# Compression contracted over 128 rows and log gates with split terms in one product, with three orders moved

## The reference, cut to what matters

```python
# compression: 31 blocks of 32 positions, 16 apart, for 2 groups of 64 channels
blocks = t[:, :, idx_c] + pe                     # (B, G, 31, 32, 64)
flat = blocks.reshape(B, G, n_cmp, L * DH)       # 32 * 64 = 2048 long
return jax.nn.silu(flat @ w1) @ w2               # w1: 2048 x 64
...
# log gates of the linear attention: rank 16
log_a = jax.nn.log_sigmoid((a_lr @ w_alpha2 + b_alpha).astype(jnp.float32)) / GLA_TAU
b = jnp.cumsum(heads(log_a, GLA_DK), axis=3)
```

## Time and profile before

| | before |
|---|---|
| median of 3 runs | 1480.3 us (1478.27 to 1482.73) |
| profiled execution, its own time | 1477.46 us |
| its span | 1475.7 us |
| PE busy | 1464.4 us (99%), 7260 matmuls |
| PEld busy | 1182.3 us (80%) |
| DVE, ACT, POOL busy | 664.9, 584.3, 653.6 us |
| granted clock | 1.0 over the whole span |

### The profile page before, as it was taken

How to read it: one execution, slowest core, us unless ns; L and a number is a source line. 1 busy time by engine, 2 the same in 40 slices (tenths; PEclk the granted TensorE clock), 3 DMA queues, 4 the chain that set the end, 5 groups by cost and what they waited for, 6 DMA issues and landing times.

```text
span 1475.7 us, 19987 instructions
## 1 busy us (share of the span) xinstructions
PE 1464.4 (99%) x7260; PEld 1182.3 (80%) x7260; DVE 664.9 (45%) x1081; ACT 584.3 (40%) x919; POOL 653.6 (44%) x304
## 2 busy tenths in 40 slices
PE   9999999999999999999999999999999999999999
PEld 7888888888878877888888886777678888888887
DVE  5214655775544276333340107988665333333000
ACT  5133332765563344333232225666654322332221
POOL 4434312772244434444444542666234444444543
PEclk9999999999999999999999999999999999999999
DMA  5522211111123222333323333321123332333333
GB/s 196 160 86 83 75 57 58 43 58 44 58 86 100 87 84 88 98 99 99 93 92 112 102 104 119 120 72 60 41 74 98 100 96 90 98 99 100 100 106 123
DMA packets 38495, 135.07 MB, mean 92 GB/s; under 512 B 4496, under 2 KB 4752, under 8 KB 38176
## 3 DMA queue, kind: packets, MB, share of 16 engines
q1 hardware_dynamic: 37248, 130.70, 27.8%
q10 hardware_dynamic: 1184, 3.51, 0.7%
HBM read 132.09 MB, written 2.10 MB: 91 GB/s over the span
## 4 chain that ended last, share of the span: by engine, by line
PE 78%; issue 13%; DVE 4%; POOL 4%; ACT 0%; DMA 0%; POOLq 0%; SPq 0%; DVEq 0%
PE bank L1149 17%; PE bank L1151 17%; PE bank L1150 17%; POOL wL L479 3%; PE bank L1500 3%; PE bank L1502 3%; PE bank L1501 3%; PE bank L1178 2%; PE bank L1180 2%; PE bank L1179 2%; DVE bank L2229 1%; PE bank L1279 1%; PE bank L1280 1%; PE bank L1281 1%; PE bank L1555 1%
## 5 line engine op out<-in xcount | busy, mean ns | idle before, releaser
L479 POOL TENSOR_TENSOR wL<-raw,wH 128x1024 fp32r<-128x1024 f32 x234 | 573.8, 2452 | 766.7 <-ACT wH L575 628.4
L575 ACT ACTIVATE wH<-raw 128x1024 fp32r<-128x1024 f32 x209 | 221.3, 1059 | 592.0 <-PE bank L1151 526.4
L1149 PE MATMUL bank<-aH,wH 128*128 128x512 f32 x920 | 359.8, 391 | 1.1 <-POOL wL L479 1.1
L1150 PE MATMUL bank<-aL,wH 128*128 128x512 f32 x920 | 358.0, 389 | 0.0
L1151 PE MATMUL bank<-aH,wL 128*128 128x512 f32 x920 | 358.0, 389 | 0.0
L1149 PEld LDWEIGHTS bank<-aH,wH 128*128 128x128 f32 x920 | 172.7, 188 | 40.7 <-POOL wL L479 2.1
L1151 PEld LDWEIGHTS bank<-aH,wL 128*128 128x128 f32 x920 | 172.7, 188 | 36.2
L1150 PEld LDWEIGHTS bank<-aL,wH 128*128 128x128 f32 x920 | 172.7, 188 | 35.9 <-issue 0.5
L1151 PE MATMUL bank<-fH,wL 128*128 128x512 f32 x352 | 137.0, 389 | 0.0
L1150 PE MATMUL bank<-fL,wH 128*128 128x512 f32 x352 | 137.0, 389 | 0.0
L1149 PE MATMUL bank<-fH,wH 128*128 128x512 f32 x352 | 136.9, 389 | 0.0
(11 more groups left out here) (332 smaller groups left out, 2010.0 us busy)
## 6 DMA issues: line engine op xcount, KB each, us to landing
raw<-in_w SPq DMA_DIRECT2D x234, 512.0 KB, 3.3
bmk<-in_bias SPq DMA_DIRECT2D x6, 512.0 KB, 4.6
out_x<-xT SPq DMA_DIRECT2D x8, 256.0 KB, 4.4
xT<-in_x SPq DMA_DIRECT2D x3, 512.0 KB, 7.3
ct<-in_ct ACTq DMA_DIRECT2D x3, 384.0 KB, 4.2
w1k<-in_w1k ACTq DMA_DIRECT2D x1, 1024.0 KB, 6.0
w1v<-in_w1v ACTq DMA_DIRECT2D x1, 1024.0 KB, 5.0
xT<-in_x SPq DMA_DIRECT2D x2, 256.0 KB, 3.5
```

The lines of the kernel that those rows point to most:

```text
L479: pool.tensor_tensor(wL[:, c_slot, :], raw[:, c_slot, :], wH[:, c_slot, :].bitcast(F32), ALU.subtract).then_inc(sem("w_lo"), 1)
L575: act.activation(wH[:, s, :], raw[:, s, :], ACT.Copy).then_inc(sem("w_hi"), 1)
L1149: pe.matmul(bank[:], hi, H[:, ka, :], start=(k == 0), stop=False)
L1150: pe.matmul(bank[:], hi, L[:, ka, :], start=False, stop=False)
```

## The change

The compression contracts two positions at once: the first 16 positions of a block lie in rows 0 to 63 and the last 16 in rows 64 to 127, so that 16 products over 128 rows replace 32 over 64 rows for each tensor and group. Both groups now use all rows and differ only in the partitions (columns of the array) that they write. `kin` is filled in eight DVE operations of 64 partitions. PE's values of group 4 are interleaved with the compression: keys, one chunk, values, one chunk, two log gates, two chunks.

The log gates become one product each in the rounded type: rows 0 to 15 hold the high parts of weight and input, rows 32 to 47 the low part of the weight by the high part of the input, rows 64 to 79 the weight rounded again by the low part of the input, the other rows zeros. ACT makes the high parts (three copies) and DVE the low parts (two subtractions) ahead of time.

In three places an order moves: on ACT in `swiglu`, `ahead(p, 1, 1)` goes ahead of `silu(0, 1)`; on DVE in the grid loop, `normed(2, 1)` goes ahead of three taps; behind the loop, `low_of_conv(3)` goes ahead of `masked_max(13)`.

```diff
@@ act, in1
+            act.wait_ge(sem("small_landed"), 16 * 5)
+            act.activation(alpha_w[0:ALPHA_ROWS], wa2, ACT.Copy).then_inc(sem("alpha_split"), 1)
+            for row in ALPHA_AT[0:2]:
+                act.activation(alpha_x[row:row + 32], pj[0:32, MISC, :], ACT.Copy).then_inc(sem("alpha_split"), 1)
             group(p, 12)
+            group(p, 16, 1)
             act.wait_ge(sem("cmp_hid"), 1)
...
+            group(p, 17, 1)
             log_gate(0)
             log_gate(1)
-            group(p, 16, 2)
-            act.wait_ge(sem("kin_ready"), 4)
+            group(p, 18, 1)
+            act.wait_ge(sem("kin_ready"), 8)
             act.wait_ge(sem("v_S"), 2)
             high_of_keys(0)
+            group(p, 19, 1)
             high_of_keys(1)
-            group(p, 18, 2)
             group(p, 20)
@@ act, swiglu
                     high_f(0, 0)
+                    ahead(p, 1, 1)
                     silu(0, 1)
-                    ahead(p, 1, 1)
                     high_f(0, 1)
@@ pe, in1
-            for i, w1 in enumerate((w1k, w1v)):
-                for l in range(CL):
-                    for g in range(NG):
-                        r = slice(g * DH, (g + 1) * DH)
-                        mm = pe.matmul(B[7][r, i * 64:i * 64 + NCMP], w1[r, l, :], kin[i][r, l, :],
-                                       start=(l == 0), stop=(l == CL - 1))
-            mm.then_inc(sem("cmp_hid"), 1)
+            def hidden_of_blocks(i, w1):
+                for b in range(CST):
+                    for g, rows in enumerate(group_rows):
+                        mm = pe.matmul(B[7][rows, i * 64:i * 64 + NCMP], w1[:, b, :], kin[:, i, b, g, :],
+                                       start=(b == 0), stop=(b == CST - 1))
+                return mm
             def log_gate(h):
-                pe.matmul(B[ALPHA_BANK[h]][:], wa2[:, h * DK:(h + 1) * DK], pj[0:RANK, MISC, :], start=True, stop=True)\
-                    .then_inc(sem("alpha_z"), 1)
+                pe.matmul(B[ALPHA_BANK[h]][:], alpha_w[0:ALPHA_ROWS, h * DK:(h + 1) * DK], alpha_x[0:ALPHA_ROWS, :],
+                          start=True, stop=True).then_inc(sem("alpha_z"), 1)
+            hidden_of_blocks(0, w1k)
+            values_by_token(4, range(0, 2))
+            hidden_of_blocks(1, w1v).then_inc(sem("cmp_hid"), 1)
+            values_by_token(4, range(2, 4))
             pe.wait_ge(sem("v_S"), 2)
+            pe.wait_ge(sem("alpha_split"), 5)
             log_gate(0)
             log_gate(1)
-            values_by_token(4)
+            values_by_token(4, range(4, KD))
@@ dve, in1
-                    dve.tensor_tensor(kin[i][:, a * CST:(a + 1) * CST, :], src, pos, ALU.add).then_inc(sem("kin_ready"), 1)
+                    for g, rows in enumerate(group_rows):
...
+                        dve.tensor_tensor(kin[group_rows[a], i, :, g, :], src, pos, ALU.add).then_inc(sem("kin_ready"), 1)
...
+            dve.wait_ge(sem("alpha_split"), 3)
+            row = ALPHA_AT[1]
+            dve.tensor_tensor(alpha_w[row:row + 32], wa2[row:row + 32], alpha_w[row:row + 32].bitcast(F32), ALU.subtract)\
+                .then_inc(sem("alpha_split"), 1)
+            dve.tensor_tensor(alpha_x[ALPHA_AT[2]:ALPHA_ROWS], pj[0:32, MISC, :], alpha_x[0:32].bitcast(F32), ALU.subtract)\
+                .then_inc(sem("alpha_split"), 1)
...
+            values_by_token(4)
             dve.memset(attnT[:], 0.0).then_inc(sem("attn_zero"), 1)
-            values_by_token(4)
@@ dve, in2
+                if SPREAD_AT.get(t) == 2:
+                    normed(2, 1)
                 taps(left)
-                if t in SPREAD_AT:
+                if SPREAD_AT.get(t, 2) < 2:
                     normed(SPREAD_AT[t], 1)
...
             silu_of_conv(3)
+            low_of_conv(3)
             masked_max(13)
-            low_of_conv(3)
```

More of the change, by code:

```diff
@@ L34 @@
 GH, DK, DV, RANK, TAU, CH = 4, 128, 256, 16, 16.0, 64
+ALPHA_AT, ALPHA_ROWS = (0, 32, 64), 96
 NCH = S // CH
@@ L239, in two_blocks_kernel @@
         spare = sb("spare", [P, S], F32, sc1)
-        wa2 = spare[0:RANK, :]
+        wa2 = spare[0:ALPHA_ROWS, :]
         kcx = sb("kcx", [P, NG, 2 * NCP], F32R, sc1)
         with ExitStack() as early:
[L243 to L246, removed]
+            sb("under_kin", [P, 2, S], F32, early)
+            kin = sb("kin", [P, 2, CST, NG, NCMP], F32, early)
+            w1k = sb("w1k", [P, CST, DH], F32, early)
+            w1v = sb("w1v", [P, CST, DH], F32, early)
+            sb("under_alpha", [P, 576], F32, early)
+            alpha_w = sb("alpha_w", [P, S], F32R, early)
+            alpha_x = sb("alpha_x", [P, S], F32R, early)
         with ExitStack() as gla:
@@ L1266, in _, with values_by_token @@
             mm.then_inc(sem("nr_T"), 1)
-            def values_by_token(g):
-                for k in range(KD):
+            def values_by_token(g, ks=range(KD)):
+                for k in ks:
                     q = p.c0 + 4 * g + k // 2
@@ L1286, in _ @@
             pe.wait_ge(sem("small_landed"), 16 * 5)
-            pe.wait_ge(sem("kin_ready"), 4)
+            pe.wait_ge(sem("kin_ready"), 8)
             pe.wait_ge(sem("v_root"), 1)
-            for i, w1 in enumerate((w1k, w1v)):
-                for l in range(CL):
-                    for g in range(NG):
-                        r = slice(g * DH, (g + 1) * DH)
-                        mm = pe.matmul(B[7][r, i * 64:i * 64 + NCMP], w1[r, l, :], kin[i][r, l, :],
-                                       start=(l == 0), stop=(l == CL - 1))
-            mm.then_inc(sem("cmp_hid"), 1)
-            def log_gate(h):
-                pe.matmul(B[ALPHA_BANK[h]][:], wa2[:, h * DK:(h + 1) * DK], pj[0:RANK, MISC, :], start=True, stop=True)\
-                    .then_inc(sem("alpha_z"), 1)
+            def hidden_of_blocks(i, w1):
[4 more added lines that the diff above has]
+                return mm
+            def log_gate(h):
+                pe.matmul(B[ALPHA_BANK[h]][:], alpha_w[0:ALPHA_ROWS, h * DK:(h + 1) * DK], alpha_x[0:ALPHA_ROWS, :],
[4 more added lines that the diff above has]
+            values_by_token(4, range(2, 4))
             pe.wait_ge(sem("v_S"), 2)
+            pe.wait_ge(sem("alpha_split"), 5)
             log_gate(0)
             log_gate(1)
-            values_by_token(4)
+            values_by_token(4, range(4, KD))
             pe.wait_ge(sem("hid_ready"), 2)
@@ L1850, in _ @@
                 for a in range(CL // CST):
-                    src = pj[:, tile, a * CST:a * CST + NCMP * CST].rearrange("p (n b) -> p b n", b=CST)
-                    pos = pv[:, PV_AT[pe_name] + a * CST:PV_AT[pe_name] + (a + 1) * CST].unsqueeze(2)\
-                        .to_broadcast([P, CST, NCMP])
-                    dve.tensor_tensor(kin[i][:, a * CST:(a + 1) * CST, :], src, pos, ALU.add).then_inc(sem("kin_ready"), 1)
+                    for g, rows in enumerate(group_rows):
+                        src = pj[rows, tile, a * CST:a * CST + NCMP * CST].rearrange("p (n b) -> p b n", b=CST)
+                        pos = pv[rows, PV_AT[pe_name] + a * CST:PV_AT[pe_name] + (a + 1) * CST].unsqueeze(2)\
+                            .to_broadcast([DH, CST, NCMP])
+                        dve.tensor_tensor(kin[group_rows[a], i, :, g, :], src, pos, ALU.add).then_inc(sem("kin_ready"), 1)
             group(2)
@@ L2479, in lay_out, with halves_in_rows @@
     pvec = np.concatenate([pvs[n] for n, _ in PV_COLS], 1)
[L2480 to L2484, removed]
+    def halves_in_rows(w1):
+        return w1.reshape(2, CST, DH, DH).transpose(0, 2, 1, 3).reshape(2 * DH, CST * DH)
+    alpha = np.zeros((ALPHA_ROWS, GH * DK), np.float32)
+    for row in ALPHA_AT:
+        alpha[row:row + RANK] = f["gla_w_alpha2"]
+    out = {"x": f["x"].T, "w": stream, "pv": pvec, "ct": constants(), "wa2": alpha,
+           "w1k": halves_in_rows(f["nsa_cmp_w1_k"]), "w1v": halves_in_rows(f["nsa_cmp_w1_v"]),
            "w2k": twice(f["nsa_cmp_w2_k"]), "w2v": twice(f["nsa_cmp_w2_v"]),
```

## The result

| | before | after |
|---|---|---|
| median | 1481.5 us (1478.27 to 1483.31, 6 runs) | 1470.3 us (1469.54 to 1471.41, 6 runs) |
| profiled execution, its own time | 1477.46 us | 1469.54 us |
| its span | 1475.7 us | 1467.6 us |
| mean granted clock of the profiled execution | 1.0 | 0.999 |

The ratio on record for these runs is 0.9935, with a 95% interval of 0.9924 to 0.9946. On 1481.5 us that is 9.6 us less, with 8.0 and 11.3 as its ends; the 8.24 us of the prediction lies inside, near the lower end. The two medians themselves differ by 11.2 us, at the upper end. The two profiled spans differ by 8.1 us.

The account below looks back on a forecast made before the run. PE, busy 99% of the span, was taken as the bound. Gains of 5.04 + 1.66 + 0.69 + 0.85 = 8.24 us took the median from 1480.3 to 1472.1 us, range 1469 to 1477.

Parts of the forecast that it names:

- The compression's price: Compression on PE: 128 records instead of 256 at the unchanged 29.6 ns each, 3.79 us instead of 7.58.
- The argument from the earlier trace: NSA values step before: paired loads start together, spanning 0.14 us, so column groups sharing all rows load at once.
- rival of groups in turn: Compression: column groups take turns loading, 55 ns a record, 3.2 us of gain gone, 1475.3 us; chance 0.14.
- rival of 114 ns a record: Compression: a product must end before the next load in the same rows, 10.8 us lost, 1482.9 us; chance 0.04.
- The block: Compression plus log gates 0 and 1 on PE, with entries and exits: 4.65 us instead of 9.69, 5.04 less.
- second entry and exit: Compression in two pieces: one more switch into and out of its products, costing 0.09 + 0.11 us.
- Gates 2 and 3: Later pair of log gates on PE: 0.45 us instead of 2.11, 1.66 us less.
- The orders: Feed-forward wait for POOL gains 0.69 us, grid wait for `normed(2, 1)` gains 0.85, `low_of_conv(3)` nothing.
- What was to be hidden: Added ACT copies, DVE subtractions and four more `kin` operations, ending at 65.2, cost nothing within existing idle times.
- margin of `b_ready`: Ahead of PE's second compression layer: gates, 7.9 us before, run 113.9 to 121.8; margin falls from 14 to 2.3 us.
- rival of a new wait: First projection: ACT or DVE slips 3.5 us past the 2.3 us margin, for `b_ready` or a chunk, 1475.6 us; chance 0.06.
- The zero point: Whole kernel: profiled execution of 1477.46 us lies 2.8 us below the median 1480.3, from which the gain was subtracted.

Follow-up runs that it names:

- experiment 7: Changed kernel with both groups in one product of 62 moving columns, keys and values in turn, 32 products in one piece; 1467.64 us, ratio to before 0.992.
- Experiment 2: Changed kernel with the 16 compression products of group 0 ahead of the 16 of group 1 instead of in turn; 1474.59 us in one run.
- experiment 5: Changed kernel with the compression in one piece, gates right behind, ACT's old order of chunks; 1469.67 us, ratio to before 0.9929.
- experiment 3: Changed kernel with plain fp32 log gates over 16 rows, the new copies and subtractions kept; 1472.07 us in one run.
- experiment 1: Kernel before with only the 128-row compression, in one piece, gates and orders as before; 1477.24 us against 1480.77, ratio 0.997.
- experiment 8: Kernel before with only the split: old products in two pieces with chunks between, gates behind; 1479.65 us, ratio 0.9995.
- experiment 4: Changed kernel with all three orders put back as before; 1472.06 us in one run.
- experiment 6: Changed kernel with ACT's first four high parts of keys ahead of log gates 0 and 1; 1473.58 us in one run.

## Why the prediction was right, step by step

**The compression's price.** Predicted 29.6 ns a record and 3.80 us in all; measured 3.98 us in two pieces (31 ns a record) and 3.85 in one (30.1). The argument from the earlier trace rows, that two column groups load at once although they share all rows, gave the right price, and the load records of experiment 7 show the same. Experiment 2 measures the other side, 57 ns a record and 3.3 us in all. So the rival of groups in turn was priced well (55 ns, 3.2 us) and didn't occur, because PE's order alternates them. The rival of 114 ns a record is excluded by both. The Trainium skill, "TensorE: Matmul & The Clock Gate", Part 3 (Packing small matmuls), says that loads overlap with matmuls only where their row groups differ. Experiment 2 disagrees: there all records use all 128 rows in either order, and alternating their columns took the price from 57 to 31 ns.

**The block.** Predicted 5.04 us less, measured 4.72. The term that was too small is the second entry and exit, put at 0.09 + 0.11 = 0.20 us: experiment 5 measures 0.45 for the split, which is 0.25 of the 0.32 missing. Each piece took 2.18 us instead of 2.10, and behind it some products start at 0.24 instead of 0.227, which the reckoning by one edge doesn't count.

**Gates 2 and 3.** Predicted 1.66, measured 1.63 by the shifts and 1.6 by experiment 3.

**The orders.** Predicted 0.69 + 0.85, measured 1.03 + 0.92. Both terms were undersized, the feed-forward's above all, because I took the wait's own time. In the trace of before, PE's timeline around the product that waits reads:

```profile
567.29 0.39 PE L1151 MATMUL bank<-aH,wL 128*128 128x512 f32 x1
...
568.71 0.40 PE L1150 MATMUL bank<-aL,wH 128*128 128x512 f32 x1
568.95 0.40 PE L1151 MATMUL bank<-aH,wL 128*128 128x512 f32 x1
```

The product behind 567.29 started at 568.37, 1.08 us on instead of 0.227: 0.85 lost. The next started 0.34 behind it and the one after 0.24, another 0.12. That is 0.97 of the 1.03. `low_of_conv(3)` was predicted at nothing and measured at nothing. The misses, 0.35 too much on the block and the gates and 0.41 too little on the orders, cancelled in the sum: 4.72 + 1.63 + 1.03 + 0.92 = 8.30 us at the four places, where 8.24 was forecast. That the sum came so close is luck; each term was right to 0.4 us.

**What was to be hidden.** `kin` takes 12.35 us in eight operations where twice 5.93 was forecast, and ended at 65.70 instead of 65.2; the next evictions follow at once, and PE doesn't wait for them. DVE's timeline after, which answers to the earlier trace rows:

```profile
53.35 12.35 DVE L1870 TENSOR_TENSOR kin<-pj,pv 64x496 f32<-64x496 f32 x8
65.73 1.29 DVE L1857 TENSOR_TENSOR pj<-bank,nr 128x512 f32<-128x512 f32 x2
```

So half the partitions save nothing in a DVE operation. The step that failed is the margin of `b_ready`: "the margin falls from 14 us to 2.3 us". The end of the gates was forecast at 121.8 and came at 123.95. The forecast moved the 7.9 us of before as one piece; in its new place the second scan met a POOL operation and took 3.37 us instead of 1.23, which is 2.14 us. PE didn't wait, so the time was right, in part by luck: the rival of a new wait was 0.56 us away and not 2.3.

**The zero point.** The profile of before on which the sum rests was an execution with a granted clock of 1.0. Of the 28 executions of before that were timed beside the experiments, 3 show 1.0 (mean 1477.8 us), 10 show 0.999 (1479.5), 12 show 0.998 (1480.8) and 3 show 0.997 (1483.7). So the 2.8 us between the profile and the median, which the prediction carried along without a cause, go with the clock. The six runs of after all show 0.999, and the mean of those of before is 0.9985. That would explain 0.7 us of the 1.4 by which the central 9.6 exceeds 8.24, but the clock is given in three digits and the interval takes in 8.24 anyway; why the medians differ by as much as 11.2 us stays open. The stretch behind compression and plain gates was seen in one of four profiles of before and in experiment 1, and in none of the two of after nor in any with rounded gates; not in experiments 3 and 8 with plain gates either. That the change makes half clock rarer at this place is supported by these counts and not settled.

## What to carry to other kernels

Small products that differ only in the columns of the array that they use can be put in turn: it took a record from 57 to 31 ns, and it leaves the rows free for a twice as long contraction. Where two streams share their weights, put them side by side in one product first: 62 moving columns cost no more than 31 beside such a load, and it gained another 1.9 us by the trace. A margin read from an old order holds only for the operations that stood beside it: when a chain moves on DVE, look at what POOL does in its new place, and when a wait is removed, count PE's restart, not only the idle time (1.03 us came back here for 0.69 of idle time).

## What the runs showed of the hardware

- **A scan on DVE and a subtraction on POOL get in each other's way.** A scan takes 1.22 us alone. Where it starts within POOL's operation of 2.4 us it ends about 1.08 us behind POOL's end: 120.58 + 3.37 = 123.95 against 120.46 + 2.41 = 122.87. The second profile of after and experiments 2 and 4 show 3.37, 3.36 and 3.36, experiment 5 3.31. Where POOL starts within the scan, it is POOL that grows; before, at 114.25, to 2.92 us instead of 2.40, in the last 0.75 us of the scan of 113.77. In the last 0.2 us of a scan it didn't grow (2.40 and 2.37 us in experiments 8 and 6). DVE's addition ahead of the scan behaves alike: 2.36 us in experiment 6 and 2.71 in experiment 7 beside POOL, 0.69 alone.
- **PE's clock falls in short stretches in which PE has no gap.** Zero to two in each of the 14 profiles, about 1.5 us lost in those behind the compression, at four places of the program. In the 4 us ahead of a stretch PE idled 0.24 to 0.26 us at three of the places and not at all behind the compression. What sets one off isn't known from these runs.
- **Plain fp32 records of 64 columns.** 30 to 31 ns each where two halves of the array alternate, in rows or in columns; 57 where they don't.
